# A two-layer hybrid model on one core: the low copies of the expert gather on ScalarE, its one-hot rows on GpSimd, and the last down product in column halves

## The reference

```python
def moe_swiglu(h, router_w, wg, wu, wd):
    logits = jnp.einsum('bsd,de->bse', h, router_w).astype(jnp.float32)
    top_val, top_idx = lax.top_k(logits, TOP_K)
    gates = jax.nn.softmax(top_val, axis=-1)
    combine = jnp.sum(jax.nn.one_hot(top_idx, N_EXPERTS, dtype=jnp.float32) * gates[..., None], axis=-2)
    out = jnp.zeros_like(h)
    for e in range(N_EXPERTS):
        out = out + combine[..., e:e + 1].astype(h.dtype) * swiglu(h, wg[e], wu[e], wd[e])
    return out
```

## Time and profile before

| | us |
|---|---|
| median of 3 runs | 1541.75 (1541.41 to 1542.61) |
| profiled execution | 1544.39 |
| its span in the trace | 1542.6 |
| PE busy | 1503.1 (97%) |
| PEld busy | 1243.0 (81%) |
| DVE busy | 1190.7 (77%) |
| ACT busy | 975.6 (63%) |
| POOL busy | 11.0 (1%) |

### The profile page before, as it was taken

The page is one execution under the profiler, slowest core; times in us unless marked ns, Lnnn a source line. Parts: engine busy times, 40 slices in busy tenths (PEclk is TensorE's granted clock), DMA queues, the critical chain, the costliest instruction groups (busy, mean ns, idle before and its releaser), DMA issues.

```text
span 1542.6 us, 19268 instructions
## 1 busy us (share of the span) xinstructions
PE 1503.1 (97%) x7347; PEld 1243.0 (81%) x7347; DVE 1190.7 (77%) x881; ACT 975.6 (63%) x742; POOL 11.0 (1%) x26
## 2 busy tenths in 40 slices
PE   7999999999999999999999999999999999999996
PEld 5987788888888678888878888887888888888885
DVE  4777454444787588898888889888889888888885
ACT  4565433344556477777767776776777777777774
POOL 2000000000000000000000000000000000000000
PEclk9999999999999999999999999999999999999998
DMA  9624555554552279999999999999999998999991
GB/s 312 217 96 139 177 191 189 189 190 137 178 177 96 96 271 387 372 361 360 376 324 336 373 375 351 369 335 327 373 366 350 372 376 316 359 365 377 355 375 61
DMA packets 190583, 437.70 MB, mean 284 GB/s; under 512 B 9328, under 2 KB 13472, under 8 KB 190384
## 3 DMA queue, kind: packets, MB, share of 16 engines
q1 hardware_dynamic: 189024, 432.90, 78.0%
q0 software_dynamic: 1056, 2.19, 0.7%
q10 hardware_dynamic: 432, 1.57, 0.3%
HBM read 435.59 MB, written 1.05 MB: 283 GB/s over the span
## 4 chain that ended last, share of the span: by engine, by line
PE 91%; DVE 4%; issue 2%; ACT 2%; DMA 1%; SPq 0%; DVEq 0%; ACTq 0%
PE ps L1219 28%; PE ps L1221 28%; PE ps L1220 28%; PE ps L1523 2%; DVE w_lo L1068 1%; DVE w_lo L760 1%; PE ps L1480 1%; PE ps L1498 1%; DMA raw<-in_w_in_dram 1%; PE ps L1499 1%; ACT w_hi L584 0%; PE ps L1282 0%; PE ps L1281 0%; PE ps L1280 0%; ACT w_hi L440 0%
## 5 line engine op out<-in xcount | busy, mean ns | idle before, releaser
L1068 DVE TENSOR_TENSOR w_lo<-raw,w_hi 128x2048 fp32r<-128x2048 f32 x333 | 754.1, 2288 | 111.9 <-ACT w_hi L584 110.9
L584 ACT ACTIVATE w_hi<-raw 128x2048 fp32r<-128x2048 f32 x332 | 630.4, 1920 | 171.7 <-PE ps L1221 171.7
L1219 PE MATMUL ps<-w_hi,aT_hi 128*128 128x512 f32 (+1 forms) x1296 | 512.8, 396 | 13.9 <-DVE w_lo L760 6.1
L1221 PE MATMUL ps<-w_hi,aT_lo 128*128 128x512 f32 (+1 forms) x1296 | 504.6, 389 | 0.0
L1220 PE MATMUL ps<-w_lo,aT_hi 128*128 128x512 f32 (+1 forms) x1296 | 503.1, 388 | 0.0
L1219 PEld LDWEIGHTS ps<-w_hi,aT_hi 128*128 128x128 f32 x1296 | 244.0, 188 | 68.3 <-issue 11.6
L1221 PEld LDWEIGHTS ps<-w_hi,aT_lo 128*128 128x128 f32 x1296 | 243.8, 188 | 53.0
L1220 PEld LDWEIGHTS ps<-w_lo,aT_hi 128*128 128x128 f32 x1296 | 244.2, 188 | 48.7
L760 DVE TENSOR_TENSOR w_lo<-raw,w_hi 128x2048 fp32r<-128x2048 f32 (+2 forms) x81 | 176.9, 2186 | 109.5 <-ACT w_hi L440 109.3
L440 ACT ACTIVATE w_hi<-raw 128x2048 fp32r<-128x2048 f32 (+2 forms) x81 | 148.0, 1830 | 117.1 <-PE ps L1221 110.8
L1219 PE MATMUL ps<-w_hi,s2T_hi 128*128 128x512 f32 x544 | 213.8, 393 | 1.5 <-DVE s2T_lo L773 1.5
(11 more groups left out here) (260 smaller groups left out, 897.3 us busy)
## 6 DMA issues: line engine op xcount, KB each, us to landing
raw<-in_moe_w_gate_dram SPq DMA_DIRECT2D x112, 1024.0 KB, 6.9
raw<-in_moe_w_up_dram SPq DMA_DIRECT2D x112, 1024.0 KB, 7.5
raw<-in_moe_w_down_dram SPq DMA_DIRECT2D x112, 1024.0 KB, 7.0
raw<-in_w_in_dram SPq DMA_DIRECT2D x20, 1024.0 KB, 6.0
raw<-in_ffn_w_gate_dram SPq DMA_DIRECT2D x14, 1024.0 KB, 5.0
raw<-in_ffn_w_up_dram SPq DMA_DIRECT2D x14, 1024.0 KB, 5.0
raw<-in_ffn_w_down_dram SPq DMA_DIRECT2D x14, 1024.0 KB, 4.7
raw<-in_w_out_dram SPq DMA_DIRECT2D x8, 1024.0 KB, 5.0
```

The source lines that it names most:

```text
L584: nc.scalar.activation(moe_hi(pos), raw[:, slot, :], ACT.Copy).then_inc(hi_ready, 1)
L1068: V.tensor_tensor(moe_lo(pos), raw[:, pos % 6, :], moe_hi(pos).bitcast(F32), ALU.subtract)\
L1219: mm(out, lhs_hi, rhs_hi, start=start, stop=False, skip_group_check=True)
L1221: return mm(out, lhs_lo, rhs_hi, start=False, stop=stop, skip_group_check=True)
```

## The change

- **Gather copies.** `gather_lo` moves from DVE to ACT, behind each `gather_hi` of the same quarter, at the entry and at the three borders.
- **One-hot rows.** DVE still writes `cur`, and builds `sel` itself only for the first pair. For the later ones GpSimd waits for `cur_ready`, runs a 128 x 1 multiplication and then builds the rows in a loop of its own.
- **Tail.** `s2T_hi` and `s2T_lo` use two halves of their buffers in turn; the transposes of the last s move between the halves of down product 13; the last down product makes column half 0 first; y is split and scattered by column halves, and the scatter has four banks (`LAST_COMB = [5, 6, 7, 0]`).

```diff
+LAST_COMB = [5, 6, 7, 0]
 # gpsimd
+            def build_sel(p, builds):
+                pool.wait_ge(cur_ready, p + 1)
+                nc.gpsimd.tensor_tensor(small[:, 0, 8:9], cur[:, 0, 0, 0:1], cur[:, 0, 0, 0:1], ALU.mult)
+                for b in range(NB):
+                    for i in range(builds):
+                        ins = nc.gpsimd.tensor_scalar(sel[:, b, i, :], iota, cur[:, 0, b, i:i + 1], None, ALU.is_equal)
+                ins.then_inc(sel_built, 1)
+            pool.wait_ge(routed, 1)
+            last = pool.value_load(n_items[0:1, 1:2], min_val=E // 2 - 1, max_val=E - 1)
+            with pool.Fori(0, last) as p:
+                build_sel(p + 1, 3)
+            build_sel(last + 1, 1)
 # scalar
+            def gather_lo(p, q):
+                act.wait_ge(gath_psum, p * 9 + (2 * q + 2))
+                nc.scalar.activation(pair_view(aT_lo, q), gath_view(2 * q + 1), ACT.Copy).then_inc(gath_lo, 1)
...
                     gather_hi(p + 1, 0)
+                    gather_lo(p + 1, 0)
                     gather_hi(p + 1, 1)
+                    gather_lo(p + 1, 1)
                     gather_hi(p + 1, 2)
+                    gather_lo(p + 1, 2)
                     sp_(6 * k)
                     gather_hi(p + 1, 3)
+                    gather_lo(p + 1, 3)
                     sel_transposed(p + 1)
...
                     sp_(6 * k - 1)
+                    evac_sT(k)
                     sel_transposed(p + 1)
-                    evac_sT(k)
-                    act.wait_ge(split_used, g0 + 6 * k)
-                    take_y()
+                    for n in range(2):
+                        act.wait_ge(y_half, n + 1)
+                        nc.scalar.activation(y_hi[:, n * 512:(n + 1) * 512], ps[:, 3 + n, :], ACT.Copy)\
+                            .then_inc(y_hi_ready, 1)
 # vector
-                    gather_lo(p + 1, 0)
-                    gather_lo(p + 1, 1)
-                    gather_lo(p + 1, 2)
                     lo(6 * k)
-                    gather_lo(p + 1, 3)
...
-                    take_y_lo(2 * p + 2)
-                    for b in range(NB):
-                        add_y(2 * p + 2, b, 0)
+                    for h in range(2):
+                        cols = slice(h * 512, (h + 1) * 512)
+                        dve.wait_ge(y_hi_ready, 2 * p + 2 + (h + 1))
+                        V.tensor_tensor(y_lo[:, cols], ps[:, 3 + h, :], y_hi[:, cols].bitcast(F32), ALU.subtract)\
+                            .then_inc(y_lo_ready, 1)
+                        for b in range(NB):
+                            dve.wait_ge(comb_psum, 4 * p + 4 + (2 * h + b + 1))
+                            xs = x[:, b, cols]
+                            ins = V.scalar_tensor_tensor(xs, ps[:, LAST_COMB[2 * h + b], :], cur[:, 1, b, 0:1], xs,
+                                                         ALU.mult, ALU.add)
 # tensor
                         down(6 * k + 2, k, 0)
+                        if not more and k == PAIR - 1:
+                            transpose_s(PAIR)
                         down(6 * k + 3, k, 1)
...
-                    transpose_s(k)
                     pe.wait_ge(sT_lo, s0 + k)
-                    down(6 * k - 2, k, 0)
-                    down(6 * k - 1, k, 1)
+                    for half in range(2):
+                        for kk in range(2):
+                            ins = last_down(half, 0, kk)
+                    ins.then_inc(y_half, 1)
                     pe.wait_ge(selT_ready, p + 2)
-                    scatter(2 * p + 2, 0, 0)
-                    scatter(2 * p + 2, 1, 0)
+                    last_down(0, 1, 0)
+                    last_down(0, 1, 1)
+                    last_down(1, 1, 0)
+                    last_scatter(0)
+                    last_down(1, 1, 1).then_inc(y_half, 1)
+                    last_scatter(1)
```

More of the change, by code:

```diff
@@ L650, in moe @@
                     gather_hi(0, q)
+                    gather_lo(0, q)
                 sel_transposed(0)
@@ L1041, in select, with select_first @@
                     .then_inc(cur_ready, 1)
-                dve.wait_ge(cur_ready, p + 1)
+            def select_first():
+                select(0, False)
+                dve.wait_ge(cur_ready, 1)
                 for b in range(NB):
-                    for i in builds:
+                    for i in range(3):
                         ins = V.tensor_scalar(sel[:, b, i, :], iota, cur[:, 0, b, i:i + 1], None, ALU.is_equal)
                 ins.then_inc(sel_built, 1)
-            def gather_lo(p, q):
-                dve.wait_ge(gath_psum, p * 9 + (2 * q + 2))
-                V.tensor_copy(pair_view(aT_lo, q), gath_view(2 * q + 1)).then_inc(gath_lo, 1)
             def add_y(n, b, i):
@@ L1112, in pair @@
                         dve.wait_ge(x_added, p * 4 + 4)
-                        select(p + 1, True, range(3) if more else range(1))
+                        select(p + 1, True)
                 k = PAIR
                 if more:
-                    gather_lo(p + 1, 0)
-                    gather_lo(p + 1, 1)
-                    gather_lo(p + 1, 2)
                     lo(6 * k)
-                    gather_lo(p + 1, 3)
                     lo(6 * k + 1)
@@ L1130, in pair @@
                     evac_sT(k)
[L1131 to L1133 removed]
+                    for h in range(2):
[8 more added lines that the diff above has]
+                                                         ALU.mult, ALU.add)
+                            if h == 1:
+                                ins.then_inc(x_added, 1)
             def moe(last):
                 g0 = MOE_BASE
[L1138 to L1140 removed]
+                select_first()
                 split(g0 + 2, 2)
@@ L1534, in down, with last_down, last_scatter @@
                             cols = slice(n * 512, (n + 1) * 512)
-                            ins = passes(ps[:, 3 + n, :], s2T_hi[:, j, :], s2T_lo[:, j, :], hi[:, kk, cols],
-                                         lo[:, kk, cols], start=first and kk == 0, stop=False)
+                            ins = passes(ps[:, 3 + n, :], s2T_hi[:, 4 * (k % 2) + j, :], s2T_lo[:, 4 * (k % 2) + j, :],
+                                         hi[:, kk, cols], lo[:, kk, cols], start=first and kk == 0, stop=False)
                     ins.then_inc(split_used, 1)
+                def last_down(half, n, kk):
+                    pos = 6 * PAIR - 2 + half
+                    slot, r = at(pos)
+                    pe.wait_ge(lo_ready[slot], r0 + (r + 1))
+                    hi, lo = (a.rearrange("p (k n) -> p k n", k=2) for a in (moe_hi(pos), moe_lo(pos)))
+                    j, cols = 4 * (PAIR % 2) + 2 * half + kk, slice(n * 512, (n + 1) * 512)
+                    return passes(ps[:, 3 + n, :], s2T_hi[:, j, :], s2T_lo[:, j, :], hi[:, kk, cols], lo[:, kk, cols],
+                                  start=False, stop=False)
+                def last_scatter(h):
+                    pe.wait_ge(y_lo_ready, 2 * p + 2 + (h + 1))
+                    cols = slice(h * 512, (h + 1) * 512)
+                    for b in range(NB):
+                        bank = LAST_COMB[2 * h + b]
+                        mm(ps[:, bank, :], selT[:, 0, b, :], y_hi[:, cols], start=True, stop=False, skip_group_check=True)
+                        mm(ps[:, bank, :], selT[:, 0, b, :], y_lo[:, cols], start=False, stop=True,
+                           skip_group_check=True).then_inc(comb_psum, 1)
                 def gate_up(k, e):
```

11 lines of the change are left out of this document (6 added, 5 removed).

## The result

The changed kernel takes 1537.49 us (median of 15 runs, 1533.78 to 1540.8). The kernel before, run 15 times beside it, takes 1545.4 us (1541.41 to 1547.76), so the ratio is 0.995 with an interval of 0.994 to 0.996: faster by 7.9 us (6.2 to 9.3 by the interval), where 7.7 were forecast. The predicted time, 1534.1, is 3.4 too low all the same, because the level of before was 3.65 above the median of three that the forecast had started from. The profiled execution of the changed kernel took 1534.68 us, with a span of 1532.9.

The account below looks back on a forecast made before the run. TensorE was taken as the bound in the expert part. Borders 2.9, tail 4.95 and entry 0 made 7.8, less 0.1 gives 7.7 us: median 1541.75 to 1534.1, range 1532.2 to 1537.5.

Parts of the forecast that it names:

- the last line of the sum: Whole kernel: profiled execution 1544.39 becomes 1536.7; as it lies 2.64 above the median 1541.75, the median becomes 1534.1 us.
- Rival A: Expert part: weight loads take the border gain back and only the tail gains, 1536.8 us; chance 0.09.
- rival B: Borders: the wait moves to ScalarE, whose low copies delay what PE needs; 1536.8, up to 1537.7 us; chance 0.07.
- Borders: Three borders between expert pairs: low copies on ScalarE free fill 4, 0.96 us each, 2.9 us gained.
- Entry: First gather, all eight copies in ScalarE's queue: taken as 0, range -0.1 to +0.6 us.
- the x2 row of the border: Timeline row at a border showing ScalarE's copies 0.47 us apart, the reason for taking the entry as 0.
- One-hot rows: Three borders: GpSimd takes 1.27 us of row building from DVE, which isn't waited for; worth 0.
- Well under 1.1 us: Sign expected in the changed profile: GpSimd's sel rows well under 1.1 us, DVE's splits beside them at 2.29.
- Rival C: Where one-hot rows are built, 974 to 981 us: GpSimd holds up DVE, kernel slower, 1548.8 us at 1.5 each; chance 0.04.
- 7 us each still hides: Upper bound for GpSimd's six rows at a border, built some 46 us before the first gather matmul reads them.
- Tail: Program end: early transposes and column halves bring the last normalization 4.95 us earlier, 1.5 of it transposes; bounds 4.2 to 5.3.
- 6H - 4.1: PE's wait at each of three borders if each GpSimd instruction of H us kept DVE still throughout; 4.1 is slack.

Follow-up runs that it names:

- run 15: Not a label but part of "run 15 times": the kernel before, unchanged, timed 15 times beside the changed kernel; 1545.4 us (1541.41 to 1547.76).

## Why the prediction was right, and where it was wrong

**The step that failed is the last line of the sum.** "It lies 2.64 above the median of the runs, 1541.75, so the median becomes 1534.1." It took three runs as the level of the kernel before, and it took the profiled execution, 1544.39, for an outlier. It was the other way round, and the 2.64 stands for nothing that the runs bear out. Over all 55 runs of before that stood beside the kernels of this study the median is 1544.44; only 9 of the 55 are at 1542.61 or less, and the three that were known (1541.41 to 1542.61) are among these. Without that correction the same sum says 1544.39 - 7.7 = 1536.7, 0.8 from what was measured, and from the median of the 15 runs of before beside it 1545.4 - 7.7 = 1537.7, 0.2 from it. The range had a term for each mechanism and none for the draw of the executions; 1537.49 lies at its very end, on a bound that was meant for rivals A and B, neither of which came. The terms for the change itself held: 2.9 and 4.95 forecast, 3.14 (with entry and stalls) and 4.95 measured.

That the level moves with the clock is seen, what moves the clock is not. In the 40 runs of before for which clock and time are both known, they correlate at -0.91, with 1.0 us per 0.001 of mean granted clock: 1548.34 at 0.988, a median of 1544.32 at 0.992 (11 runs), 1542.27 at 0.995 (3 runs). For the changed kernel's 15 runs it is -0.93 and 1.2 us. And in eight profiled executions the tail is within 0.03 us of one of three values, by the kernel's version, the expert stretch within 0.2 of one of two (0.4 in the kernel with the low copies alone, named above), while the stretch ahead ranges from 532.88 to 537.57. The Trainium skill (TensorE: Matmul & The Clock Gate, Part 1: The HAM clock gate) says that the number of slow matmuls at a kernel's start varies from run to run and puts the loss under 1% of a typical span; the runs here agree in size, with a spread of 0.2 to 0.5%, and show slow matmuls in the middle of the work too (near 80 and 450 us, in windows in which PE was busy throughout). What decides it in a given execution stays open.

**Borders.** Forecast 2.9, with fills 0.48 apart: they are, and the stretch is 3.14 shorter with entry and stalls in it. ACT's queue behaved as written, the split behind the copies starts half a microsecond sooner against the fills than it did, and nobody waits for it (rival B is out).

**Entry.** Forecast 0, range -0.1 to +0.6. From the first gather matmul to the first scatter it is 23.03 us against 23.13. The eight copies follow at 0.48 although each lasts 0.59 to 0.64: the x2 row of the border was the right one to go by.

**One-hot rows.** Worth 0, as forecast, and by the right reason, the slack of DVE. The price per instruction was bounded from 0.21 to 7 and is 0.58 undisturbed, 1.32 in the mean. "Well under 1.1 us" is therefore wrong. Rival C's estimate for six rows, near 3 us (by its factor 2.5), is low as well: undisturbed they take 3.50, 2.8 times DVE's 1.27, and beside the splits 7.62. "7 us each still hides", 42 us in all, is borne out: with 58 us PE waits 12.3, so the limit is near 46.

**Tail.** Forecast 4.95 (4.2 to 5.3), measured 4.95. The split between its two parts was off by 0.16 either way. The forecast of one gap of about 1.4 us before the last scatter is row by row what came (1.41).

**Rival A**, the weight loads take the border gain back: out. The mean rose from 359 to 360 GB/s, landings are as before and no engine waits for one:

```profile
DMA to landing us min/median/max: 4.7/7.1/9.6
```

The bound of 358 in the Trainium skill (SBUF — State Buffer, Summary: rules for kernel authors), by which this rival would have been the forecast, is none with one core at work: 385 GB/s stand in the window of after from 15 to 25 us.

**Rival C**, GpSimd holds up DVE: half right. Exclusion there is, and a row that meets a split waits until the split is over. By the rival's formula, 6H - 4.1 with H = 1.32, PE would have lost 3.8 us at each border. It lost none: the splits at 973.87 and 976.62 start 0.03 us after ACT has ended their high parts, and last 2.29 and 2.31. The step that fails is "kept DVE still for all of its time". Most of H is GpSimd's own waiting for DVE, and of the 0.60 us of an undisturbed row only about 0.2 (the estimate above) keep DVE out.

The Trainium skill (SBUF — State Buffer, Who interferes with whom) says that a two-input DVE instruction and a GpSimd one that reads SBUF contend, which the 2.16 us of a one-element product shows. It also says that issue order decides who blocks. The run with six times the rows agrees, with splits of 2.34 to 2.44 us where a row had over 0.4 still to come. In the changed kernel no row well under way had more than 0.30 to come, and so the rule costs nothing there: the row from 973.44 to 974.03 was under way when the split began at 973.87, and the split took 2.29. DVE lost at most 0.02 us an instruction in the changed kernel and 0.15 with six times the rows, GpSimd whole splits. There is a slower case, though, that no rival of mine named: rows that come late. It begins where GpSimd needs 46 us in place of 9.8.

## What to carry to other kernels

Before a difference of half a per cent is turned into a time, ask how the profiled execution and the few known runs lie to each other; where they differ by a third of the effect, either may be the odd one, and the range needs a term for it. An instruction that stands in an in-order queue behind a long one costs what the long one takes, so move it to the engine that has just produced its neighbour, and price it by the spacing of such instructions in a row, not by their length. Where two engines exclude each other, ask for how long one instruction of each keeps the other out: here the engine with the short ones paid nearly all, so it is how late its results come that has to be budgeted. At the end of a program, where nothing overlaps any more, go through the chain and cut the last product so that its first half is evacuated beside its second.

## What the runs showed of the hardware

GpSimd builds a 128x128 fp32 comparison in 0.58 us when DVE splits no weights, and in 1.3 to 2.3 (means of six in a row) beside DVE's splits of 2.29 us. The splits give up at most 0.15, and only where a row has over 0.39 us still to come. A multiplication of one element per partition takes GpSimd 0.19 to 0.20 us in the first case and up to 2.26 in the second. ACT's copies of 512 columns last 0.60 us and start 0.48 apart. The granted clock drops to its lower level for some us in places where kernels do identical work (near 80 and 450 us, with PE busy), in some executions and not in others, and a PE that stood for 12 us restarts at it.
